# State-space sums of the second block: the y matmuls of two heads issued alternately into the two halves of the output partitions

## What is computed

```python
CB = jnp.einsum("bclgn,bcsgn->bclsg", Cc, Bc)            # once per group g
Lmat = jnp.exp(jnp.where(tri, seg, -jnp.inf))            # per head, seg = differences of cumulated log decays
Y_diag = jnp.einsum("bclsgr,bcsgrp->bclgrp", CB[..., None] * Lmat, X)   # per head
...
y = direction(dt_f, ..., False) + direction(dt_b, ..., True) + D_skip * xh
```

## Time and profile before

| | |
|---|---|
| median of 3 runs | 2598.07 us (2596.22 to 2601.36) |
| the profiled execution, its own time | 2602.04 us |
| span of the profile | 2600.3 us |
| mean granted TensorE clock | 0.955 of full |
| TensorE busy | 2424.7 us, 93% |
| VectorE busy | 1557.8 us, 60% |
| ScalarE busy | 1081.0 us, 42% |

### The profile page before, as it was taken

The page is one execution under the profiler, slowest core; times in us unless marked ns, Lnnn a source line. Parts: engine busy times, 40 slices in busy tenths (PEclk is TensorE's granted clock), DMA queues, the critical chain, the costliest instruction groups (busy, mean ns, idle before and its releaser), DMA issues.

```text
span 2600.3 us, 43623 instructions
## 1 busy us (share of the span) xinstructions
PE 2424.7 (93%) x18842; PEld 2314.6 (89%) x18842; DVE 1557.8 (60%) x2610; ACT 1081.0 (42%) x1428; POOL 395.7 (15%) x254
## 2 busy tenths in 40 slices
PE   2898999999999996999999799995999899999997
PEld 2898999999999995999999677795998899888997
DVE  4332555555456556349999888686654536666454
ACT  2322444554444443334333444443443445455442
POOL 1000000000000000037777000470000012221000
PEclk7887999999999998989999899998999999999999
DMA  4632444555556652545555243455455465555562
GB/s 138 164 104 90 124 145 131 167 162 173 168 179 185 188 182 79 171 130 174 167 168 187 93 135 117 145 173 141 144 178 162 124 181 166 162 155 155 162 189 71
DMA packets 409468, 391.91 MB, mean 151 GB/s; under 512 B 45464, under 2 KB 403160, under 8 KB 408954
## 3 DMA queue, kind: packets, MB, share of 16 engines
q1 hardware_dynamic: 373406, 381.69, 48.0%
q10 hardware_dynamic: 35872, 7.46, 1.6%
HBM read 386.77 MB, written 5.95 MB: 151 GB/s over the span
## 4 chain that ended last, share of the span: by engine, by line
PE 88%; DVE 7%; ACT 2%; ACTq 2%; DMA 1%; issue 1%; SPq 0%; DVEq 0%; PEldq 0%
PE ps L408 25%; PE ps L410 24%; PE ps L409 24%; PE ps L1956 3%; PE ps L2022 1%; PE ps L481 1%; DVE wlo L361 1%; PE ps L1798 1%; DMA raw<-in_w_in_dram 1%; DVE arena L1524 1%; PE ps L1731 1%; PE ps L1999 1%; PE ps L2011 1%; DVE arena L507 1%; DVE ps L1440 1%; PE ps L1823 1%
## 5 line engine op out<-in xcount | busy, mean ns | idle before, releaser
L408 PE MATMUL ps<-op_hi,whi 128*128 128x256 f32 (+1 forms) x5440 | 1579.1, 290 | 54.8 <-DVE op_lo L453 30.1
L410 PE MATMUL ps<-op_hi,wlo 128*128 128x256 f32 (+1 forms) x5440 | 1560.4, 287 | 0.0
L409 PE MATMUL ps<-op_lo,whi 128*128 128x256 f32 (+1 forms) x5440 | 1557.6, 286 | 0.0
L354 ACT ACTIVATE whi<-raw 128x1024 fp32r<-128x1024 f32 (+1 forms) x688 | 721.3, 1054 | 1064.3 <-PE ps L410 962.2
L408 PEld LDWEIGHTS ps<-op_hi,whi 128*128 128x128 f32 x5440 | 1037.3, 191 | 92.4 <-issue 82.2
L361 DVE TENSOR_TENSOR wlo<-raw,whi 128x1024 fp32r<-128x1024 f32 x560 | 678.4, 1227 | 650.2 <-ACT whi L354 649.9
L410 PEld LDWEIGHTS ps<-op_hi,wlo 128*128 128x128 f32 x5440 | 1037.2, 191 | 0.0
L409 PEld LDWEIGHTS ps<-op_lo,whi 128*128 128x128 f32 x5440 | 1035.9, 190 | 0.5 <-issue 0.2
L361 POOL TENSOR_TENSOR wlo<-raw,whi 128x1024 fp32r<-128x1024 f32 x128 | 311.0, 2432 | 1366.8 <-ACT whi L354 1366.7
L1440 DVE SCALAR_TENSOR_TENSOR ps<-arena,param_cols,ps 128x257 f32<-128x257 f32 (+6 forms) x448 | 182.9, 487 | 0.0
L702 POOL TENSOR_TENSOR arena<-arena 128x256 f32<-128x256 f32 x64 | 64.9, 1033 | 277.6 <-DMA arena<-bias_by_column 277.6
(11 more groups left out here) (269 smaller groups left out, 1544.0 us busy)
## 6 DMA issues: line engine op xcount, KB each, us to landing
raw<-in_e_w_in_dram SPq DMA_DIRECT2D x96, 1024.0 KB, 5.4
raw<-in_w_in_dram SPq DMA_DIRECT2D x84, 1024.0 KB, 5.2
raw<-in_o_w_in_dram SPq DMA_DIRECT2D x64, 1024.0 KB, 6.0
raw<-in_e_w_out_dram SPq DMA_DIRECT2D x32, 1024.0 KB, 5.3
raw<-in_w_out_dram SPq DMA_DIRECT2D x16, 1024.0 KB, 5.3
raw<-in_w_ple_gate_dram SPq DMA_DIRECT2D x16, 1024.0 KB, 5.3
raw<-in_o_w_out_dram SPq DMA_DIRECT2D x16, 1024.0 KB, 5.3
arena<-cum_rows SPq DMA_DIRECT2D x16, 544.0 KB, 6.0
```

Source lines behind the costliest of these rows:

```text
L354: nc.scalar.activation(half_view(whi[c % 2], c, n), half_view(raw[c % RING], c, n), ACT.Copy).then_inc(hi_ready, 1)
L408: nc.tensor.matmul(o, wh, xh, start=(i % cpp == 0 and k == 0), stop=False)
L409: nc.tensor.matmul(o, wh, xl, start=False, stop=False)
L410: mm = nc.tensor.matmul(o, wl, xh, start=False, stop=(i % cpp == cpp - 1 and k == 7))
```

## The change

The four passes of the loop over heads become two passes over pairs. In a pass TensorE first does its halves of chunks as before, then waits until both heads of the pair are weighed, then issues the twelve matmuls piece by piece: head 0's piece, head 1's same piece, head 0's next piece, and so on. Each head's last matmul still counts up `y_psum`. No other engine's program is touched.

```diff
-                    for h in range(4):
-                        for i in {0: (1,), 2: (2, 3)}.get(h, ()):
+                    for k in range(2):
+                        for i in ((1,), (2, 3))[k]:
                             multiply(pe, s, 2 * G + i // 2, i % 2, T2)
-                        pe.wait_ge(S("w_ready"), G * 4 + (h + 1))
-                        o = HD * (h % 2)
+                        pe.wait_ge(S("w_ready"), G * 4 + 2 * k + 2)
                         for i, (d, st, lo, hi, at) in enumerate(SSD_COLS):
                             n = P if st < 2 else META
-                            mm = T.matmul(ps[o:o + HD, 4 + h // 2, lo:hi], XNAT[0:n, st, HD * h:HD * h + HD], SEG[0:n, h % 2, at:at + hi - lo],
-                                          start=(i == 0), stop=(i == len(SSD_COLS) - 1))
-                        mm.then_inc(S("y_psum"), 1)
+                            for b in range(2):
+                                h = 2 * k + b
+                                mm = T.matmul(ps[HD * b:HD * b + HD, 4 + k, lo:hi], XNAT[0:n, st, HD * h:HD * h + HD], SEG[0:n, b, at:at + hi - lo],
+                                              start=(i == 0), stop=(i == len(SSD_COLS) - 1))
+                                if i == len(SSD_COLS) - 1:
+                                    mm.then_inc(S("y_psum"), 1)
```

## The result

The changed kernel takes 2620.39 us (median of 4 runs, 2616.78 to 2621.43), the kernel before, run beside it, 2599.49 us. The ratio is 1.008, with a 95% interval of 1.0064 to 1.0096: 20.9 us slower. The profiled execution took 2620.63 us, its span is 2618.9 us. The ratios of the experiments leave out two executions that took more than twice as long, one of the kernel before (5903.57 us) and one of the kernel with a third buffer (6328.65 us).

What follows compares the result with a forecast made beforehand. The prediction took TensorE, busy 93%, as the bound, with VectorE's weighing before each pair in the chain. Lateness +10.5 us and clock falls +17.6 made +28 us, 2598 to 2626 us; 8-in-10 range 2604 to 2641.

Steps and rivals of the forecast that it cites:

- Two heads at once: In the y matmuls, both heads of a pair run side by side, 2.25 us a pair instead of 4.42.
- First pair: First pair of a group: starts at T + 11.74, T being when TensorE leaves the previous second pair; gains 0.27 us.
- Second pair: Second pair of a group: starts at E + 10.05, E being when TensorE leaves the first pair; loses 1.63 us.
- The sum without the clock: Over the stretch of the sums: +1.36 us a group times 7, +9.5, and +1 for the last group, +10.5 us.
- The clock: TensorE's clock falls in four or five of seven 3.8 us waits before second pairs, 3.9 us each, +17.6 us.
- Two signs: In the after trace: group period 26.3 us where the clock stays up, about 30 us where it falls.
- No overlap: Rival at the y matmuls: the two heads do not overlap, a pair keeps 4.42 us, +42 us or more; 4%.
- faster: Rival: TensorE sets the pace, 16 pairs at 2.2 us less, 2563 us; needs head 3 weighed by E + 6.24; 5%.
- no change: Rival: second-pair losses a us smaller than worked out and no clock falls, within 5 us; 9%.
- Late, but no falls: Rival: pairs late as worked out but the clock never falls, +10.5 us, 2608 us; 25%.

Runs made afterwards that it cites:

- third buffer: Changed kernel with a third buffer for head 2's differences, so they need not wait for the first pair; 2594.91 us, ratio 0.9986.
- the earlier low parts: Changed kernel with chunk 2G + 2's high parts made after head 1's exponential and low parts after head 1's weighing; 2586.89 us, ratio 0.9947.
- the kernel that was kept busy in the waits: Changed kernel with unused matmuls filling TensorE's waits, 16 before each first pair and 30 before each second; 2610.26 us, ratio 1.0041.
- the best kernel: Changed kernel with chunk 2G + 2's parts and chunk 2G + 3's low parts earlier, chunk 2G's first half after CB matmuls and transposes; 2572.7 us.

## Why the prediction came out as it did

**Two heads at once.** 2.25 us a pair was forecast from `n_sums`; 2.22 was measured. Right.

**First pair.** Forecast to start at T + 11.74, measured T + 11.77, and the wait before it 2.07 us. The gain of 0.27 us against T + 14.26 came as worked out. Right.

**Second pair.** Forecast E + 10.05, measured E + 10.04, with each step on VectorE and ScalarE at its time in the rows of the result. The third buffer and the earlier low parts each remove one link of that chain and shorten it by what the link was forecast to cost (12.27 to 10.01 and to 9.16 us), so the mechanism is shown, and not only read from the rows.

**The sum without the clock.** Forecast +10.5 us; with the clock held the stretch takes 10.4 us more, and the kernel 11 us. The last group, taken as +1, is 1.2 of it (21.7 us from the start of its first pair to the end of its second, 20.5 before). Right.

**The clock.** That the waits would bring falls of the clock was right. The size was not. Forecast: falls in four or five of the seven long waits, 3.9 us each, 17.6 us. Measured: four falls in the long waits, and 11.3 us in all. This is the term that was mis-sized, and it makes up the difference between 2626 and 2620. It failed in two ways that partly cancel. The price was taken from the one fall that the trace before has among the y matmuls, whose low clock lasted over the whole half chunk behind it; of the four falls in long waits one was like that (18.26 us to the next pair instead of 13.98, 4.3 us) and three ended within the pair (15.34 or 15.35, 1.4 us each). The number, four, fits the four or five forecast. And the sum gave the waits of about 2 us no falls, because an idle stretch of 2.7 us elsewhere had passed without one: four falls lay there, three at 0.8 us each and the last group's at 0.5. With 4.3 + 3 x 1.4 + 3 x 0.8 + 0.5 = 11.4 us the account closes. That the two errors went against each other is luck: the price put 9 us too much into the sum, and the falls left out of it 3 us too little.

The trace of before also had a row against that reading, 15 us behind the one that was read, between two sets of transposes at the end of the program (TensorE's timeline):

```profile
2592.49 3.29 PE L2052 MATMUL ps<-ident,arena 128*128 128x128 f32 x16 [2.15 <-DVE arena L1704]
```

The clock was at 1.00 through this idle time of 2.15 us and fell to 0.50 at 2593.21, 0.7 us after it.

Two signs that the prediction named came out otherwise by this error. A period of about 30 us for a group with a fall was seen once (30.5 us, group 0 to group 1); the six others took 27.0 to 27.6. And no group was without a fall, so the period of 26.3 us appears only where the waits are filled (12.27 + 13.98). The lower end of the range, 2604 us "without falls", also doesn't fit the prediction's own sum, which gives 2608 for that case.

**The rivals.** "No overlap", "faster" and "no change" are out by the rows above. "Late, but no falls" is what the kernel that was kept busy in the waits shows, 2610 us against the 2608 named. The faster rival was a question of when head 3 is weighed. It was said to turn the sign at E + 8.6 and to need E + 6.24 in full. The third buffer (second pair 7.8 us after the end of the first, 4 us faster than before) and the earlier parts (6.9, 14 us faster) lie on the other side of that point, as said.

## What to carry to other kernels

Packing two small matmuls side by side needs both operands at once, so it replaces a wait for the first by a wait for the last and releases both buffers only at the end. Work out, from the rows of the engine that makes the operands, when the second of the pair is ready and who waits for the first one's buffer; if that engine becomes the busier one once the matmuls are packed (here VectorE, busy 20.5 us a group against 19.5 of TensorE in the best kernel), give it other work to do beside the pair in the same edit. Pack first where both operands are ready anyway: here the second pair alone gained 7 us and the first alone lost 20.

A fall of the clock has no fixed price: count which work stands behind it. One that led into a wait of 3.7 us cost 0.8 us here, one with a pair and a half chunk behind it 4.2.

## What the runs showed of the hardware that was not expected

- An idle time of 2.07 us before the y matmuls, which have 64 output partitions and some of them 16 rows, was followed by a fall of the granted clock in four of seven groups, 1.1 to 1.3 us after the matmuls had begun. The idle stretch of 2.65 us in front of full-width matmuls near the end of the program was not, in this trace or in any other of this case. Whether that is for the matmuls behind the wait or for the moment at which the wait comes, no run here tells; it stays open.
- A fall needs no idle time at all. In the trace of before the clock fell at 1132.31 us, in a part of the program that the change doesn't touch, though TensorE had had no gap between its matmuls for over 12 us. The last 34 of them, over 3.6 us, had outputs of 128x64, those before them of 128x272. All thirteen traces have this fall, with no gap in the 12 us before it. The stretches before and behind it, in the columns of rows 3:

```profile
1120.00:1132.30 12.30, 12.30 (x104) 12.30 (x103) 2.92 (x4) 3.78 (x5) 4.69 (x2) 1.00 0.56 171
1132.30:1140.00 7.70, 7.70 (x39) 7.70 (x38) 0.00 (x0) 0.00 (x0) 0.05 (x1) 0.50 0.45 138
```

- Taking the short waits away went with a fall at each of the long ones in that trace (seven of seven in groups 0 to 6 instead of four), with dearer falls (four of the seven cost 4.0 to 4.2 us instead of one of four), and with a kernel 12 us slower.
- In the last group VectorE's twelve weighings stretch from 3.89 to 10.30 us while GpSimd makes low parts, and to 12.43 us in the changed kernel. The Trainium skill, "GPSIMD Engine Reference", section "Specifications", says that the two share their SBUF interfaces and contend where a VectorE instruction has two inputs there, as the weighing has; the trace agrees. The experiment with the low parts made earlier shows it too: in its last group the twelve take 3.90 us with GpSimd idle, and eight weighings of heads 0 and 1, which take 2.54 us elsewhere, take 6.82 beside GpSimd's work. In the changed kernel TensorE waits 6.98 us before that group's second pair, where it waited 3.38 in the middle of the pair before.
